# Modulation rows of a two-block transformer kernel: six per feed-forward stage and three per mixer, with ScalarE rounding the hidden products

## The reference

```python
cond = silu(c)
for l in range(2):
    mod = cond @ w_ada[l] + b_ada[l]          # nine rows of 1024
    sh1, sc1, g1, sh2, sc2, g2, sh3, sc3, g3 = split(mod, 9)
    y = swiglu(x * (1 + sc1) + sh1, gate, up, down)   # 1024 -> 2816 -> 1024
    x = post_norm(x, y, g1, 0.5, ...)
    y = token_mixer(x * (1 + sc2) + sh2, w_in, w_out)
    x = post_norm(x, y, g2, 1.0, ...)
    y = swiglu(x * (1 + sc3) + sh3, gate, up, down)
    x = post_norm(x, y, g3, 0.5, ...)
```

## Time and profile before

| | us |
|---|---|
| median of 3 runs | 2330.91 (2329.78 to 2332.93) |
| the profiled execution's own time | 2332.08 |
| its span | 2330.3 |
| PE busy | 2021.3 |
| DVE busy | 1116.1 |
| ACT busy | 538.0 |
| POOL busy | 71.2 |

### The profile page before, as it was taken

One profiled execution on the slowest core, in us unless ns is written; L12 is line 12 of the kernel. 1 busy time (PEld: TensorE's weight loads), 2 busy tenths in 40 slices (PEclk: granted clock), 3 DMA queues, 4 the chain that ended last, 5 costly groups with the idle time before them and its releaser, 6 DMA issues.

```text
span 2330.3 us, 34856 instructions
## 1 busy us (share of the span) xinstructions
PE 2021.3 (87%) x13572; PEld 1372.8 (59%) x13572; DVE 1116.1 (48%) x1723; ACT 538.0 (23%) x830; POOL 71.2 (3%) x109
## 2 busy tenths in 40 slices
PE   7999999999999999999999976666669997666665
PEld 5999456999899745799886532222239642222222
DVE  3877777878877777887743310000017421000001
ACT  3333133433434223343333100000014210000000
POOL 0000000000000000000300000000000000000000
PEclk9999999999999999999999989999899998999998
DMA  9987865888688776788754799999997789999997
GB/s 345 330 296 259 318 242 216 295 311 302 228 287 312 254 294 247 258 302 319 246 217 146 307 422 421 422 422 422 422 404 260 288 338 422 421 422 422 422 422 319
DMA packets 240443, 757.49 MB, mean 325 GB/s; under 512 B 14016, under 2 KB 124256, under 8 KB 193136
## 3 DMA queue, kind: packets, MB, share of 16 engines
q1 hardware_dynamic: 233248, 737.33, 82.4%
q0 software_dynamic: 6864, 19.00, 2.7%
q10 hardware_dynamic: 256, 0.13, 0.0%
HBM read 755.22 MB, written 1.18 MB: 325 GB/s over the span
## 4 chain that ended last, share of the span: by engine, by line
PE 57%; DMA 32%; DVE 5%; SPq 3%; ACT 1%; DVEq 1%; issue 1%; ACTq 0%
DMA W<-in_w_exp_down 28%; PE psum L868 22%; PE psum L880 10%; PE psum L923 4%; PE psum L942 4%; PE psum L1394 3%; PE psum L1333 2%; PE psum L1300 2%; SPq L590 2%; PE psum L1148 1%; PE psum L785 1%; DMA W<-in_w_conv_in 1%; DMA W_mod<-in_mod_w 1%; PE psum L1314 1%; DMA W<-in_w_exp_up 1%
## 5 line engine op out<-in xcount | busy, mean ns | idle before, releaser
L868 PEld LDWEIGHTS psum<-parts 128*128 128x128 f32 x4224 | 517.8, 192 | 9.1 <-issue 1.9
L868 PE MATMUL psum<-parts 128*128 128x256 f32 x4224 | 521.0, 283 | 1.1 <-ACT parts L1430 0.8
L1300 PE MATMUL psum<-W,scr 128*32 128x512 f32 x1920 | 276.2, 699 | 174.6 <-DMA W<-in_w_exp_up 171.5
L2327 DVE TENSOR_TENSOR scr<-scr,psum 128x256 f32<-128x256 f32 x32 | 13.5, 421 | 551.1 <-ACT scr L1698 551.1
L1771 DVE SCALAR_TENSOR_TENSOR mod_acc<-W_mod,cond,mod_acc 128x1024 f32<-128x1024 f32 x196 | 251.8, 1285 | 47.4 <-issue 27.5
L880 PE MATMUL psum<-parts 128*128 128x512 f32 x1056 | 258.0, 393 | 0.2 <-DVE parts L1966 0.2
L1300 PEld LDWEIGHTS psum<-W,scr 128*32 128x32 f32 x1920 | 59.7, 118 | 319.0 <-issue 182.5
L1940 DVE TENSOR_TENSOR parts<-W,parts 128x1024 fp32r<-128x1024 f32 x176 | 207.2, 1219 | 69.3 <-ACT parts L1486 69.3
L880 PEld LDWEIGHTS psum<-parts 128*128 128x128 f32 x1056 | 192.6, 188 | 45.7 <-DVE parts L1953 7.8
L785 PE MATMUL psum<-k_ones,k_ident 128*128 128x256 f32 x736 | 206.6, 413 | 0.0
L785 PEld LDWEIGHTS psum<-k_ones,k_ident 128*128 128x128 f32 x736 | 135.8, 200 | 105.3 <-issue 91.5
(11 more groups left out here) (325 smaller groups left out, 1679.8 us busy)
## 6 DMA issues: line engine op xcount, KB each, us to landing
W<-in_w_exp_down SPq DMA_DIRECT2D x128, 1024.0 KB, 26.5
W_mod<-in_mod_w SPq DMA_DIRECT2D x123, 1024.0 KB, 6.5
W<-in_w_exp_up SPq DMA_DIRECT2D x120, 1024.0 KB, 26.1
W<-in_w_exp_gate SPq DMA_DIRECT2D x120, 1024.0 KB, 25.1
W<-in_ffn_w_gate SPq DMA_DIRECT2D x44, 1024.0 KB, 9.0
W<-in_ffn_w_up SPq DMA_DIRECT2D x44, 1024.0 KB, 11.6
W<-in_ffn_w_down SPq DMA_DIRECT2D x44, 1024.0 KB, 10.3
W<-in_w_in SPq DMA_DIRECT2D x24, 1024.0 KB, 8.5
```

The costliest lines, as they stand in the source:

```text
L868: ins = pe.matmul(psum[:, 4 + t % 2, S * g:S * g + S], w[:, t % 2, g, kc, :], u[:, kc, :], start=(n == 0 and kc == 0), stop=(n == 2 and kc ...
L1300: ins = pe.matmul(psum[32 * q:32 * q + 32, 4, :].rearrange("p (g n) -> p g n", g=2), x, w[:, :, q, :], start=(b == 0), stop=(b == KC - 1), ...
```

## The change

The 32 rows are dealt out anew: six in each feed-forward stage (FFN_ROWS = PAIRS + 1) and three in each mixer. The sixth row's four chunks go into slot 6 of W, which no feed-forward stage uses, one in each of the first four turns; SP waits with each for extra_freed, which DVE raises when the chunk before is used up. DVE adds its blocks at t = 4 in uT's first half (extra_acc), which lies idle in a feed-forward stage. PE sums it among the last down products, DVE adds its bias behind the last tile's products, and ACT stores it. The mixers' rows 2 and 4 of before go; rows 0, 1 and 3 stay as 0, 1 and 2. The second part: the product of silu and up is rounded by ACT (high_hidden), between DVE's multiplication (hidden) and its subtraction (low_hidden), and DVE does one block of a row between the two. Three semaphores are new: h_made, h_high, extra_freed. The diff, cut:

```diff
-JOBS_LAYER = 3 * PAIRS
+FFN_ROWS = PAIRS + 1
+MIX_ROWS = 3
+JOBS_LAYER = 2 * FFN_ROWS + MIX_ROWS
...
-MIX_BANK = (3, 3, 3, 1, 6)
-MIX_CHUNKS = {2: (0, 2), 6: (2, 6), 8: (6, 10), 9: (10, 12), 10: (12, 14), 11: (14, 16), 12: (16, 18)}
+MIX_BANK = (3, 3, 1)
+MIX_CHUNKS = {2: (0, 2), 6: (2, 6), 8: (6, 8), 9: (8, 10), 10: (10, 12)}
+EXTRA_SLOT = 6
...
+def ffn_job(l, k):
+    return l * JOBS_LAYER + FIRST_JOBS + k * (FFN_ROWS + MIX_ROWS)
...
@@ SP, ffn_stream
                 if k == 1:
-                    for c in (2, 3):
-                        mod_chunk(l * JOBS_LAYER + (FIRST_JOBS + 2 * PAIRS - 1), c, PAIRS - 1)
                     sp.wait_ge(m_pe.s, m_pe.at("out", l))
...
                         step_weights(l, k, r + 1, i * 2 + (r + 1), base + i * 4 + 2 * r, lambda: chunk(2 * r))
                         chunk(2 * r + 1)
+                        if r == 0 and not last:
+                            sp.wait_ge(extra_freed, i + (4 * (2 * l + k) + 1))
+                            job = ffn_job(l, k) + PAIRS
+                            src = A["mod_w"][job:job + 1, ds(i * 256, 256), :]
+                            sp.dma_start(part(W[:, EXTRA_SLOT, :], 0, 2, D), src.rearrange("a (k p) n -> p (a k) n", p=P)
+                                         ).then_inc(landed[EXTRA_SLOT], 16)
...
@@ SP, mixer
                     if u < 2:
                         sp.wait_ge(pn_x, l * 6 + 2)
+                        sp.wait_ge(extra_freed, 8 * l + 5)
...
@@ PE, ffn
                 down_ready(TILES - 2)
                 down_rows(TILES - 2, 0)
+                mod_sum(ffn_job(l, k) + PAIRS, (extra_freed, 4 * extras_before(l, k) + 5), acc=extra_acc)
                 down_rows(TILES - 2, 1, (0, 2))
                 down_ready(TILES - 1)
...
-                pe.wait_ge(mod_taken, l * JOBS_LAYER + (FIRST_JOBS + PAIRS + 2 * PAIRS * k))
+                pe.wait_ge(mod_taken, ffn_job(l, k) + FFN_ROWS)
...
@@ PE, mixer
                 heads_turned(5, 7)
                 scores(0)
-                row_sum(2)
                 project(0, 1, 1)
...
                 pe.wait_ge(m_act.s, m_act.at("ev11", l))
-                row_sum(3)
+                row_sum(2)
                 second(3)
...
                 times_rows(y_now, at, 0, (0, 1, 2, 3), order).then_inc(acc_t0, 1)
-                row_sum(4)
                 times_rows(y_now, at, 1, (0, 1, 2, 3), order, (0,)).then_inc(acc_half, 1)
...
@@ ACT, ffn
+                def high_hidden(t, i=0):
+                    act.wait_ge(h_made, f0 + i * 4 + t)
+                    if t >= 2:
+                        act.wait_ge(pe_down, f0 + i * 4 + (t - 1))
+                    act.activation(h_hi[:, t % 2, :], h_now[:, t % 2, :], copy).then_inc(h_high, 1)
...
                         silu(t, i)
+                        high_hidden(t, i)
                         if t == 4:
-                            mod_row(l * JOBS_LAYER + i + (FIRST_JOBS + 2 * PAIRS * k))
+                            mod_row(i + ffn_job(l, k))
                 high_down(TILES - 1)
                 if then is not None:
                     high_gate_up(*then, 0)
                 silu(TILES - 1)
+                high_hidden(TILES - 1)
+                mod_row(ffn_job(l, k) + PAIRS)
                 if then is not None:
                     high_gate_up(*then, 1)
                 roots_next()
...
@@ DVE, ffn
                     dve.wait_ge(act_silu, f0 + i * 4 + (t + 1))
-                    if t >= 1:
+                    dve.tensor_tensor(h_now[:, t % 2, :], silu_g[:, t % 2, :], psum[:, 4 + t % 2, S:2 * S], mul).then_inc(h_made, 1)
+
+                def low_hidden(t, i=0):
+
+                    dve.wait_ge(h_high, f0 + i * 4 + t)
+                    if t >= 2:
                         dve.wait_ge(pe_down, f0 + i * 4 + (t - 1))
-                    h_, hi, lo = h_now[:, t % 2, :], h_hi[:, t % 2, :], h_lo[:, t % 2, :]
-                    dve.tensor_tensor(h_, silu_g[:, t % 2, :], psum[:, 4 + t % 2, S:2 * S], mul)
-                    dve.drain()
-                    dve.tensor_copy(hi, h_)
-                    dve.drain()
-                    dve.tensor_tensor(lo, h_, hi.bitcast(F32), sub).then_inc(dve_h, 1)
+                    dve.tensor_tensor(h_lo[:, t % 2, :], h_now[:, t % 2, :], h_hi[:, t % 2, :].bitcast(F32), sub).then_inc(dve_h, 1)
...
                         if t < 4:
-                            mod_blocks(job, done, 3 * t - 3, min(3 * t, KC))
+                            mod_blocks(job, done, 3 * t - 3, 3 * t - 2, extras_before(l, k))
+                            low_hidden(t, i)
+                            mod_blocks(job, done, 3 * t - 2, min(3 * t, KC), extras_before(l, k))
                         else:
-                            mod_row(job, (pe_mod, done + 2), odd=2 * l + 2 * k)
+                            mod_row(job, (pe_mod, done + 2), odd=odd_before(l, k))
+                            if not last:
+                                extra_block(i, 0)
+                            low_hidden(t, i)
+                            if not last:
+                                extra_block(i, 1)
+
+                def extra_block(i, kk):
...
+                    dve.drain()
+                    if kk == 0:
+                        dve.wait_ge(landed[EXTRA_SLOT], (i + (l * LAYER_FILLS[EXTRA_SLOT] + 7 * k + 1)) * 16)
+                    ins = dve.scalar_tensor_tensor(extra_acc, w, col, extra_acc, mul, add)
+                    if kk:
+                        ins.then_inc(extra_freed, 1)
+                dve.memset(extra_acc, 0.0)
...
                 hidden(TILES - 1)
+                low_hidden(TILES - 1)
+                job = ffn_job(l, k) + PAIRS
+                mod_row(job, (pe_mod, job - FIRST_JOBS + 2), 6, None, mix_bias[1], 3 * l + 2 * k + 1)
                 if then is not None:
                     low_gate_up(*then, 1)
...
@@ DVE, mixer and behind it
                 mixer_row(l, 0)
-                mixer_blocks(2, 0, 4)
                 mixer_row(l, 1)
                 heads(3, 7)
-                mixer_blocks(2, 4, 8)
...
-                mixer_blocks(4, 0, 4)
                 plus_bias(3 * l + 1)
...
-                mixer_blocks(4, 4, KC)
...
                 for t in range(2):
                     low_gate_up(l, 1, t)
-                mixer_row(l, 4)
```

More of the change, by code:

```diff
@@ L190, in build @@
         y_tok = tmp
+        extra_acc = uT[:, 0:4, :].rearrange("p a b -> p (a b)")
         first_mod = [W_mod[:, 0, :], W_mod[:, 1, :]] + [W[:, s, :] for s in (6, 7, 3, 4, 5)] + [W_mod[:, 0, :]]
@@ L351, in build @@
         dve_h = sem("dve_hidden")
+        h_made = sem("hidden_multiplied")
+        h_high = sem("hidden_high")
+        extra_freed = sem("extra_mod_chunk_summed")
         pe_down = sem("pe_down")
@@ L456, in chunk_of, with mod_chunk @@
                 return A["mod_w"][ds(job, 1), 256 * c:256 * c + 256, :].rearrange("a (k p) n -> p (a k) n", p=P)
-            def mod_chunk(job, c, row=None):
-                sp.wait_ge(mod_freed[c % 2], 2 * job + c // 2)
+            def mod_chunk(job, c, extras, row=None):
+                sp.wait_ge(mod_freed[c % 2], 2 * (job - extras) + c // 2)
                 if c == 3:
@@ L544, in _ @@
             sp.wait_ge(m_pe.s, m_pe.at("out", LAYERS - 1))
+            sp.wait_ge(extra_freed, 8 * LAYERS + 1)
             for g in (2, 0, 1, 3, 4):
@@ L1043, in mixer @@
                 project(1, 1, 1)
-                pe.wait_ge(mod_taken, l * JOBS_LAYER + (FIRST_JOBS + 2 * PAIRS - 2))
+                pe.wait_ge(mod_taken, mix_job(l) + 2)
                 values(1)
@@ L1531, in row_out @@
                 def row_out(n):
-                    mod_row(l * JOBS_LAYER + (FIRST_JOBS + PAIRS + n))
+                    mod_row(mix_job(l) + n)
                 def heads(g, bank):
@@ L1593, in mixer @@
                 stick(3)
-                row_out(3)
+                row_out(2)
                 evacuate(2, 1, 0)
@@ L1624, in _ @@
                 norm_turn(3 * l + 2, 4 * l + 3, split=True)
-                mod_row(l * JOBS_LAYER + (FIRST_JOBS + 2 * PAIRS - 1))
                 ffn(l, 1, (1, 0) if l == 0 else None)
@@ L1755, in _, with mod_blocks @@
             mul, add, sub = ALU.mult, ALU.add, ALU.subtract
-            def mod_blocks(job, done, b0, b1, acc=mod_acc):
+            def mod_blocks(job, done, b0, b1, extras, acc=mod_acc):
                 for b in range(b0, b1):
@@ L1970, in ffn, with four @@
                 hidden(0)
-                with dve.Fori(0, PAIRS) as i:
+                low_hidden(0)
+                def four(i, last=False):
+                    job, done = i + ffn_job(l, k), i + (ffn_job(l, k) - FIRST_JOBS)
                     for t in range(1, 5):
@@ L1975, in ffn @@
                         hidden(t, i)
-                        job = l * JOBS_LAYER + i + (FIRST_JOBS + 2 * PAIRS * k)
-                        done = l * JOBS_LAYER + i + 2 * PAIRS * k
                         if t < 4:
-                            mod_blocks(job, done, 3 * t - 3, min(3 * t, KC))
```

(27 more changed lines are left out.)

50 lines of the change are left out of this document (31 added, 19 removed).

## The result

The changed kernel takes 2345.84 us (median of 4 runs, 2343.57 to 2348.28) against 2330.98 for the kernel before (4 runs): 14.9 us slower, ratio 1.0064, 95% interval 1.0050 to 1.0077. The forecast was 2342.6, with a range of 2333.5 to 2349. The profiled execution took 2345.72 us with a span of 2343.9, 13.6 more than the span before.

What follows compares the result with a forecast made beforehand. PE was taken to bound feed-forward stages and mixers, other engines only the stage boundaries. F1 and F3 +1.6, F2 +3.2, F4 +10.4 and mixers -3.5 make +11.7 on 2330.91: 2342.6 us, range 2333.5 to 2349.

Steps and rivals of the forecast that it cites:

- Loop: Feed-forward turns: the extra DVE products, ACT's rounding and the new transfer are covered by slack; turn stays 34.78 us, cost 0.
- Rival 3: Inside feed-forward turns, coupling of DVE, ACT and DVE delays each tile: 0.2 x 88 = 17.6 us more, 2360; chance 0.07.
- Sixth sums of F1 and F3: At the ends of F1 and F3, PE's sum of the sixth row costs 0.78 us each, +1.6 together.
- F2's end: ACT's rounding of the next stage's weights waits behind the product's rounding and the sixth row's store: +3.2 us, bounds +2.5 and +5.
- F4's end: Row 31, a context row, is now stored last, so its store and column load delay ACT and PE: +10.4 us.
- the loaded rows: Profile rows of small transfers under DMA load: store 5.3 us, columns 7.3; used for F4's end, giving +10.4.
- the quiet ones: Profile rows of small transfers without DMA load: store 1.9 us, columns 3.1; would give +2.8 at F4's end.
- Rival 1: At F4's end the small transfers are quick despite load, or the chain has slack: +4 in total, 2335.0; chance 0.13.
- The constants: Behind F4 in POOL's queue: loaded 13 us later, DVE wants them by 1182, so they stay hidden.
- Mixers: M1 and M2 each lose two row sums and start the end norm earlier: -1.73 us per mixer, -3.5 for both.
- Rival 2: Mixers gain 5.1 us each, -10.1 for both, if DVE's lateness spaces PE; kernel not slower, 2328.4; chance 0.07.
- The new transfer: The sixth row's chunk in SP's queue delays gate weights in the feed-forward loop, covered by about 3 us: cost 0.

Runs made afterwards that it cites:

- the quiet run: Changed kernel, but SP holds the last two w_mix_in transfers and all behind them until the context's columns are loaded; 2339.12 us, ratio 1.0042.

## Why the prediction was right, and where it was not

The direction, the main place of the loss (behind F4) and the size were right: 11.7 forecast, 14.9 measured, 13.6 in the trace. One loss, in F4's first turn, wasn't foreseen. By its own steps:

- **Loop**: 0 forecast, 34.78 us per turn measured. The rounding's price on ACT, taken as 0.384, was 0.42; no turn feels it: with the rounding alone F1, F3 and F4 have their old length to 0.01 us. Rival 3 is out. The wait of PE for DVE in F4's first turn looks like its sign, but it stands in the kernel without the rounding too.
- **Sixth sums of F1 and F3**: 1.6 forecast, 0.81 + 0.79.
- **F2's end**: 3.2 forecast, 2.61. The step was right in its parts, but their sum was not: I let the row queue behind the rounding and counted both. Alone they cost 1.1 and 2.6, and 2.6 together. The size, 0.6 off, was near because the row alone is most of it.
- **F4's end**: 10.4 forecast; 0.8 in F4 and 10.37 behind it, 11.2. The step that decided the whole forecast was to take the loaded rows and not the quiet ones, and the quiet run confirms both ends: 11.2 under load, 3.2 without. Rival 1 is out. The constants, forecast to stay hidden, did not reach the end of the kernel, though DVE waited for them.
- **Mixers**: -3.5 forecast, -6.6 in the first pair of traces, of which 4.9 are the rows and 1.7 the clock. The term was mis-sized by 1.4. M1's norm starts right with acc_t0, as forecast: DVE now waits 3.7 us for PE ahead of it. The second half of the norm came 1.2 earlier and not 1.0. And the row sum in the middle had waited 0.4 us for DVE's addition, a wait that the prediction doesn't have; with five rows it was 0.4 to 1.5 in all six mixers, with three rows it was absent in fifteen of eighteen. Rival 2's full 5.1 per mixer didn't come: the 2.0 us wait stayed, as forecast. Its sign, over 3 us per mixer, was met in M1 alone, and there by the clock.
- **The new transfer: the step that failed.** I looked for its collision in the steady turn, at the gate weights, and found 3 us of cover. It came in F4's first turn, right after a mixer, where seven transfers already stood in one burst, and what came late was the loop's own chunk in W_mod, not the new chunk: 11.7 to 12.7 us after its issue in place of 8.8. The price was 4.0 us in the first trace and 1.5 to 1.7 in the five others, where the prediction had 0. Only the steady turn was looked at. F2, which also stands behind a mixer, shows no such wait.

Two errors of opposite sign (+4.0 for the chunk, -3.1 for the mixers, 1.7 of it the clock's, for which the forecast had no term) made the total look better than its parts; that much of the fit is luck.

## What to carry to other kernels

Before a unit of work is moved to the end of a queue, ask who reads it first: here the row that the next stage wants was made the last one, and a chain of store and load that had been hidden stood open for 10 us; making another row last cost nothing. A transfer that is covered in the steady turn has to be checked in the first turn behind a stage boundary too, where the bursts are. The rows that left the mixers brought 5 us; the sums at the stages' ends and three waits at boundaries cost more than three times that (19 us in the first pair of traces).

## What the runs showed of the hardware that was not expected

- The same small store and load, with the same code around them, took 1.9 and 2.8 us at a DMA share of 0.02 and 0.26, and 5.8 and 6.6 at 1.05 to 1.10.
- The second block, which no edit touches, has two lengths. From its mixer's first product to the end it took 1165.5 to 1165.8 us in the five traces whose granted clock in 1260 to 1300 was 1.00, and 1168.9 to 1170.1 in the six where it was 0.83 to 0.87 (1167.8 in one with 0.96); both kernels have both lengths. Up to 103 us into the block DVE's steps stand within 0.3 us of each other, but for single ones early on in the kernels whose constants come late; 22 us later the kernels with the lowered clock are 4.2 to 5.5 us behind. What sets it off is open. Two stretches of the changed kernel, first trace and second:

```profile
1260.00:1300.00 40.00, 39.36 (x130) 25.34 (x128) 16.93 (x39) 9.94 (x24) 4.07 (x5) 0.83 0.58 205
```

```profile
1260.00:1300.00 40.00, 39.00 (x173) 23.83 (x175) 17.93 (x49) 8.97 (x24) 4.07 (x5) 1.00 0.60 211
```

That is about 3.5 us, 0.15% of the kernel, with one lowering of the clock: two single executions can't be compared below that, but their stages can.
